# The first layer norm of a two-layer decoder trunk: tile 0 alone on VectorE, tile 1 on ScalarE and GpSimd, norm vectors spread by TensorE, first weight block in quarters

## The reference

```python
def _layer_norm(x, g, b):
    mu = jnp.mean(xf, axis=-1, keepdims=True)
    var = jnp.mean(jnp.square(xf - mu), axis=-1, keepdims=True)
    y = (xf - mu) * lax.rsqrt(var + LN_EPS)
    return (y * g + b).astype(x.dtype)

x = _layer_norm(x, ln_in_g, ln_in_b)
for l in range(DEPTH):
    hcat = jnp.einsum('bsd,de->bse', x, w_in[l])   # D_IN = 6662 columns
    ...
```

## Time and profile before

| | |
|---|---|
| median of three runs | 871.85 us |
| the profiled execution | 871.45 us |
| its span, first to last instruction | 869.7 us |
| mean granted TensorE clock | 0.998 |

### The profile page before, as it was taken

How to read it: one execution, slowest core, us unless ns; L and a number is a source line. 1 busy time by engine, 2 the same in 40 slices (tenths; PEclk the granted TensorE clock), 3 DMA queues, 4 the chain that set the end, 5 groups by cost and what they waited for, 6 DMA issues and landing times.

```text
span 869.7 us, 10886 instructions
## 1 busy us (share of the span) xinstructions
PE 847.2 (97%) x4280; PEld 703.0 (81%) x4280; DVE 514.9 (59%) x729; ACT 406.1 (47%) x553; POOL 56.4 (6%) x86
## 2 busy tenths in 40 slices
PE   7999999999999999999999999999999899999995
PEld 7878888888877888888878889888888688888884
DVE  6755465555896555445675656463778764555436
ACT  6665555453355344444337655564443444343430
POOL 0022321000000000000000414200000000000000
PEclk9999999999999999999999999999999999999999
DMA  7774443356537655665437443435754576556501
GB/s 273 240 260 135 133 133 122 122 184 238 183 130 244 217 184 194 193 194 162 141 110 241 145 158 100 135 114 184 236 176 139 189 250 208 188 177 194 194 1 49
DMA packets 93618, 149.36 MB, mean 172 GB/s; under 512 B 3584, under 2 KB 52992, under 8 KB 93568
## 3 DMA queue, kind: packets, MB, share of 16 engines
q1 hardware_dynamic: 93568, 148.67, 52.4%
HBM read 147.60 MB, written 1.05 MB: 171 GB/s over the span
## 4 chain that ended last, share of the span: by engine, by line
PE 88%; DVE 8%; DMA 2%; ACT 2%; issue 1%; DVEq 0%; ACTq 0%
PE bank L1116 78%; DVE w_lo L913 3%; PE bank L1131 3%; PE bank L1175 3%; PE bank L1207 2%; DMA raw<-in_w_in 1%; PE bank L1195 1%; PE bank L1141 1%; DVE stats L1031 1%; ACT w_hi L802 1%; DVE x L1076 1%; DVE x L1028 1%; DVE x L1073 1%; DVE act_lo L919 1%; DVE newton L1048 0%
## 5 line engine op out<-in xcount | busy, mean ns | idle before, releaser
L913 DVE TENSOR_TENSOR w_lo<-raw,w_hi 128x2048 fp32r<-128x2048 f32 (+3 forms) x143 | 309.5, 2169 | 91.5 <-ACT w_hi L802 91.0
L1116 PE MATMUL bank<-w_hi,act_hi 128*128 128x512 f32 (+2 forms) x864 | 341.8, 396 | 0.6 <-DVE act_lo L919 0.6
L1116 PE MATMUL bank<-w_hi,act_lo 128*128 128x512 f32 (+2 forms) x864 | 332.4, 385 | 0.0
L1116 PE MATMUL bank<-w_lo,act_hi 128*128 128x512 f32 (+2 forms) x864 | 331.4, 384 | 0.0
L802 ACT CAST w_hi<-raw 128x2048 fp32r<-128x2048 f32 (+3 forms) x143 | 257.5, 1803 | 123.9 <-PE bank L1116 98.8
L1116 PEld LDWEIGHTS bank<-w_hi,act_lo 128*128 128x128 f32 x864 | 162.3, 188 | 32.9
L1116 PEld LDWEIGHTS bank<-w_hi,act_hi 128*128 128x128 f32 x864 | 162.6, 188 | 30.3 <-DVE act_lo L919 0.9
L1116 PEld LDWEIGHTS bank<-w_lo,act_hi 128*128 128x128 f32 x864 | 162.8, 188 | 28.6
L1116 PE MATMUL bank<-w_hi,y_hi 128*128 128x512 f32 x240 | 95.2, 397 | 0.0
L1116 PE MATMUL bank<-w_hi,y_lo 128*128 128x512 f32 x240 | 93.7, 390 | 0.0
L1116 PE MATMUL bank<-w_lo,y_hi 128*128 128x512 f32 x240 | 93.5, 390 | 0.0
(11 more groups left out here) (96 smaller groups left out, 576.5 us busy)
## 6 DMA issues: line engine op xcount, KB each, us to landing
raw<-in_w_in SPq DMA_DIRECT2D x47, 1024.0 KB, 5.2
raw<-in_w_gate SPq DMA_DIRECT2D x44, 512.0 KB, 3.9
raw<-in_w_up SPq DMA_DIRECT2D x44, 512.0 KB, 5.0
raw<-in_w_down SPq DMA_DIRECT2D x22, 1024.0 KB, 4.9
raw<-in_w_o SPq DMA_DIRECT2D x8, 1024.0 KB, 5.2
raw<-in_w_in SPq DMA_DIRECT2D x4, 768.0 KB, 4.5
raw<-in_w_pa SPq DMA_DIRECT2D x4, 768.0 KB, 4.3
raw<-in_w_pc SPq DMA_DIRECT2D x4, 768.0 KB, 4.4
```

The lines of the kernel that those rows point to most:

```text
L913: dve.tensor_tensor(weights(w_lo, i, HI_SLOTS), weights(raw, i, RAW_SLOTS), weights(w_hi, i, HI_SLOTS).bitcast(F32), ALU.subtract).then_in ...
L1116: ins = pe.matmul(bank[use[0]][:, 0:width], a, w[:, k, c0:c0 + width], start=start and k == 0 and p == 0, stop=stop and k == nk - 1 and p ...
```

## The change

The plan's beginning is written anew. SyncE loads tile 0, the two norm vectors as one row on one partition, the first quarter, the identity, the second quarter, tile 1, the third and fourth quarter, and then piece 4. TensorE runs 8 dummies, then multiplies a row of ones (one partition) with the norm vectors, 512 columns at a time, which puts gain and bias on all partitions in banks 2 to 5 (plain float32). VectorE computes tile 0 alone: the statistics, one inverse root by `pow` on GpSimd (with one Newton step behind it), gain and bias from the banks. Tile 1 is summed by ScalarE with an accumulating ACTIVATE, its mean, variance, root and shift are made by nine instructions of one column on GpSimd, ScalarE squares and then normalises it, and VectorE applies gain and bias (`second_affine`). The step "affine", the two broadcast loads and the ACTIVATEs of L815 are gone. The first block is four pieces of quarter size; all later pieces are the same as before under a number one higher.

```diff
-WARM = (48, 16)
+WARM = (8, 6, 14)
+QUARTERS = 4
...
+def slot_before(i, n_slots):
+
+    if i < QUARTERS // 2 + n_slots:
+        return None
+    if i < QUARTERS + n_slots:
+        return 2 * (i - n_slots - QUARTERS // 2) + 1
+    return i - n_slots
...
-    statistics({t: None for t in range(TT)}, 1)
-    scale(0)
+    norm[0] = TT
+    norm_n.update({t: t + 1 for t in range(TT)})
+    spread_rows = [[bank(2 + 2 * a + j) for j in range(2)] for a in range(2)]
+    plan.append(("warm", WARM[0]))
+    plan.append(("spread_rows", spread_rows))
+    plan.append(("warm", WARM[1]))
+    plan.append(("first_norm", spread_rows))
     split_hi()
     split_lo()
     split_hi()
-    plan.append(("warm", WARM[0]))
+    plan.append(("second_sum",))
     turn_x(0, 0)
     split_lo()
-    plan.append(("warm", WARM[1]))
-    scale(1)
+    plan.append(("second_squares",))
+    turn_x(0, 1)
     split_hi()
     split_lo()
-    turn_x(0, 1)
+    plan.append(("second_rows",))
+    split_hi()
+    split_lo()
+    plan.append(("warm", WARM[2]))
+    plan.append(("second_affine", spread_rows))
...
                     if (c, t) == (0, 1):
-                        for _ in range(HI_SLOTS - 2):
+                        split_hi()
+                        turn_x(1, 0, 1)
+                        for _ in range(HI_SLOTS - 3):
...
+            sp.dma_start(x[0][:, :], d["x"][0:P, :]).then_inc(x_loaded[0], 16)
+            sp.dma_start(norm_rows, d["norms"]).then_inc(norms_loaded, 16)
+            norms, put_off = TT, None
...
+                    if i == 0:
+                        sp.dma_start(tables[:, 0:P], d["tables"][:, 0:P]).then_inc(ident_loaded, 16)
                     if i == 1:
-                        sp.dma_start(tables[:, 0:P], d["tables"][:, 0:P]).then_inc(ident_loaded, 16)
-                        sp.dma_start(norm_cols[:, :, :].rearrange("p a k -> p (a k)"), d["norms"]
-                                     ).then_inc(norms_loaded, 16)
+                        sp.dma_start(x[1][:, :], d["x"][P:2 * P, :]).then_inc(x_loaded[1], 16)
 
                     if put_off is not None:
                         put_off -= 1
                         if put_off == 0:
                             load_gain_bias(norms // TT)
                             put_off = None
-                    if i == 4:
-                        load_gain_bias(0)
...
+                elif step[0] == "first_norm":
+                    pool.wait_ge(var_ready, 1)
+                    pool.tensor_tensor(rstd[:, 0:1], var_eps[:, 0:1], exponent[:, :], ALU.pow).then_inc(root_ready, 1)
+                elif step[0] == "second_sum":
+                    pool.wait_ge(sum_ready, 1)
+                    pool.tensor_scalar(neg_mean[:, :], row_sum[:, :], -1.0 / D_MODEL, None,
+                                       ALU.mult).then_inc(mean_ready, 1)
+                elif step[0] == "second_squares":
+                    v, r, h, z = (m[:, 1:2] for m in (var_eps, rstd, half_var, newton))
+                    pool.wait_ge(squares_ready, 1)
+                    link(pool.tensor_scalar(v, square_sum[:, :], 1.0 / D_MODEL, LN_EPS, ALU.mult, ALU.add))
+                    link(pool.tensor_tensor(r, v, exponent[:, :], ALU.pow))
+                    link(pool.tensor_scalar(h, v, -0.5, None, ALU.mult))
+                    link(pool.tensor_tensor(z, r, r, ALU.mult))
+                    link(pool.tensor_tensor(z, z, h, ALU.mult))
+                    link(pool.tensor_scalar(z, z, 1.5, None, ALU.add))
+                    link(pool.tensor_tensor(r, r, z, ALU.mult))
+                    pool.wait_ge(mean_ready, 1)
+                    pool.tensor_tensor(shift[:, :], neg_mean[:, :], r, ALU.mult).then_inc(shift_ready, 1)
...
-                    if src == "first":
-                        if idx == 1:
-                            act.wait_ge(norms_loaded, 16)
-                        source_rows = first_rows[dk // 4]
-                        if t:
-                            act.wait_ge(drained[first_use[dk][0]], first_use[dk][1])
-                        first_use[dk] = (b, n)
-                        for k in range(nk):
-                            ins = act.activation(source_rows[:, k * P:(k + 1) * P], bank[b][:, k * P:(k + 1) * P],
-                                                 ACT.Identity, bias=norm_cols[:, 1, dk + k:dk + k + 1],
-                                                 scale=norm_cols[:, 0, dk + k:dk + k + 1])
-                        link(ins)
...
+                elif kind == "second_sum":
+                    act.wait_ge(x_loaded[1], 16)
+                    act.activation(merged[1][:, :], x[1][:, :], ACT.Identity,
+                                   accum_out=row_sum[:, :]).then_inc(sum_ready, 1)
+                elif kind == "second_squares":
+                    act.wait_ge(mean_ready, 1)
+                    act.activation(merged[1][:, :], x[1][:, :], ACT.Square, bias=neg_mean[:, :],
+                                   accum_out=square_sum[:, :]).then_inc(squares_ready, 1)
+                elif kind == "second_rows":
+                    act.wait_ge(squares_ready, 1)
+                    act.wait_ge(shift_ready, 1)
+                    act.activation(merged[1][:, :], x[1][:, :], ACT.Identity, bias=shift[:, :],
+                                   scale=rstd[:, 1:2]).then_inc(centred, 1)
...
-                elif kind == "affine":
-                    _, t, (b, n) = step
-                    dve.wait_ge(gb_loaded, 32)
-                    dve.wait_ge(filled[b], n)
-                    link(dve.tensor_tensor(x[t][:, :], x[t][:, :], gain_bias[:, 0, :], ALU.mult))
-                    link(dve.tensor_tensor(x[t][:, :], x[t][:, :], gain_bias[:, 1, :], ALU.add))
...
+                elif kind == "first_norm":
+                    _, (gain, bias) = step
+                    dve.wait_ge(x_loaded[0], 16)
                     for nh in range(2):
-                        xh = x[t][:, nh * NW:(nh + 1) * NW]
-                        dve.tensor_scalar(xh, xh, mean_var[:, t, 0:1], rstd[:, t:t + 1], ALU.subtract,
-                                          ALU.mult).then_inc(x_ready, 1)
+                        mark(dve.bn_stats(stats[:, 0, nh, :], x[0][:, nh * NW:(nh + 1) * NW]))
+                    settle()
+                    link(dve.bn_aggr(mean_var[:, 0, :], stats[:, 0, :, :]))
+                    dve.tensor_scalar(var_eps[:, 0:1], mean_var[:, 0, 1:2], LN_EPS, None,
+                                      ALU.add).then_inc(var_ready, 1)
+                    mark(dve.tensor_scalar(half_var[:, 0:1], mean_var[:, 0, 1:2], LN_EPS, -0.5, ALU.add, ALU.mult))
+                    for nh, (b, n) in enumerate(gain):
+                        xh = x[0][:, nh * NW:(nh + 1) * NW]
+                        dve.wait_ge(filled[b], n)
+                        mark(dve.scalar_tensor_tensor(out=xh, in0=xh, scalar=mean_var[:, 0, 0:1], in1=bank[b][:, :],
+                                                      op0=ALU.subtract, op1=ALU.mult))
+                    settle()
+                    dve.wait_ge(root_ready, 1)
+                    link(dve.scalar_tensor_tensor(out=newton[:, 0:1], in0=rstd[:, 0:1], scalar=half_var[:, 0:1],
+                                                  in1=rstd[:, 0:1], op0=ALU.mult, op1=ALU.mult))
+                    link(dve.scalar_tensor_tensor(out=rstd[:, 0:1], in0=newton[:, 0:1], scalar=1.5, in1=rstd[:, 0:1],
+                                                  op0=ALU.add, op1=ALU.mult))
+                    for nh, (b, n) in enumerate(bias):
+                        xh = x[0][:, nh * NW:(nh + 1) * NW]
+                        dve.wait_ge(filled[b], n)
+                        dve.scalar_tensor_tensor(out=xh, in0=xh, scalar=rstd[:, 0:1], in1=bank[b][:, :], op0=ALU.mult,
+                                                 op1=ALU.add).then_inc(x_ready, 1)
+                    dve.wait_ge(x_ready, 2)
+                elif kind == "second_affine":
+                    _, (gain, bias) = step
+                    dve.wait_ge(centred, 1)
+                    for nh in range(2):
+                        half = slice(nh * NW, (nh + 1) * NW)
+                        dve.tensor_tensor(x[1][:, half], merged[1][:, half], bank[gain[nh][0]][:, :],
+                                          ALU.mult).then_inc(drained[gain[nh][0]], 1)
+                        dve.wait_ge(drained[gain[nh][0]], gain[nh][1])
+                        dve.tensor_tensor(x[1][:, half], x[1][:, half], bank[bias[nh][0]][:, :],
+                                          ALU.add).then_inc(x_ready, 1)
+                    dve.wait_ge(x_ready, 2 * TT)
+                    for spare, (b, n) in zip((shift, square_sum), bias):
+                        dve.memset(spare[:, :], 0.0).then_inc(drained[b], 1)
...
+                elif kind == "spread_rows":
+                    pe.wait_ge(norms_loaded, 16)
+                    pe.wait_ge(ones_ready, 1)
+                    for a, uses in enumerate(step[1]):
```

(26 more changed lines are left out.)

88 lines of the change are left out of this document (44 added, 44 removed).

## The result

The changed kernel takes 877.92 us (median; 876.05 to 878.88), the kernel before, timed beside it, 871.98 us. The ratio is 1.0063, with a 95% interval of 1.0051 to 1.0076: 0.63% slower. It is estimated from the runs of both kernels and is not the quotient of the two medians, which lie 5.9 us apart. The profiled execution took 877.86 us with a span of 876.1 us, 6.4 us more than the span before (869.7). The mean granted clock of the four executions differs (0.994, 0.991, 0.996 and 0.998 for 876.1, 877.1, 876.2 and 874.3 us of span); the profiled one is the first.

The account below looks back on a forecast made before the run. TensorE, busy 97% of the span, bounds the kernel, so tile 1's first product with weights was the mark: 3.9 us later, less 1.7 given back, +2.2 on the 871.85 median makes 874.1 us; range 870.8 to 876.8.

Parts of the forecast that it names:

- Tile 0, the spreading: Start, TensorE's four norm-vector products: over at 10.05 us, first product with weights near 13.3 instead of 14.21.
- I take the same 3.9 us from there: Spreading products: TensorE's clock stays low for 3.9 us from 4.65, when unbroken work starts; later products run faster.
- Tile 1's chain: Tile 1 on ScalarE, GpSimd, VectorE: shift ready at 17.4, first product at 26.3 instead of 22.37, 3.9 us later.
- The two meetings: GpSimd's tile 1 steps stopped by VectorE's `w_lo` of the second and third quarter, costing 0.55 and 1.15 us.
- The clock falls in the holes: Rival, chance 0.10: TensorE's clock drops in its waits between about 17.6 and 26.3 us, losing 1.95 us: 876.0.
- the hole of 1.44 us: Kernel before: TensorE's wait ending at 19.15; the 0.22 us spacing behind it showed no fall of the clock.
- Given back: Ahead of the attention scores: the later tile 1 start closes two existing TensorE waits, returning 1.7 us.
- the holes: Kernel before: TensorE waits of 0.29 us at 54.08 and 1.41 us at 58.95, forecast to close.
- GpSimd's first arithmetic late: Rival, chance 0.07: GpSimd's first arithmetic is delayed at tile 0's root; 5 us late gives 876.8 us.
- The range: Forecast span of the whole time, 870.8 to 876.8 us, leaving out the faster case and most of the late GpSimd.
- the likeliest case: Whole kernel: tile 1's delay less the closed waits, +2.2 us, 874.1 us; chance 0.43, own range 873.1 to 875.5.
- the supply of weights: Chain of `w_lo` steps and loads ending in the waits at 54 and 59 us; reaches the scores by 60.65 at latest.

Follow-up runs that it names:

- a1_first: Changed kernel with 24 dummies instead of 8 at the start, ahead of the norm-vector products: 876.82 us, ratio to the kernel before 1.0046.
- d1: Changed kernel, still 8 dummies first, with the norm-vector products made over all 128 rows instead of one: 875.9 us, ratio to the kernel before 1.0053.
- b1: Changed kernel with norm-vector products over 128 rows instead of one and 24 dummies first instead of 8: 874.83 us, ratio to the kernel before 1.0034.
- b2: Changed kernel without the five GpSimd instructions of tile 1's Newton step: 875.73 us, ratio to the kernel before 1.0043.
- a3: Changed kernel with the fourth quarter's cast and low part ahead of ScalarE's third pass over tile 1: 875.68 us, ratio to the kernel before 1.0036.
- a2: Changed kernel with 14 dummies ahead of the fourth quarter's products and 14 behind tile 1's turns: 876.27 us, ratio to the kernel before 1.0041.
- c1: Changed kernel with 128-row norm-vector products, 24 dummies first, and the fourth quarter's cast and low part ahead of ScalarE's third pass: 871.31 us, ratio 0.9992.
- b3: Kernel before with only the first block's weights in four quarter pieces instead of two quarters and a half: 871.38 us, ratio 0.9997.
- b4: Changed kernel: 24 dummies first, fourth quarter's cast before third pass, tile 1's turned halves before whole-piece cast, 6 and 8 dummies around its turns: 874.71 us.
- c3: Changed kernel: 128-row products, 24 dummies first, fourth quarter's cast before third pass, no tile 1 Newton step, turned halves before cast, 6 dummies between turns: 870.63 us.

## Why the prediction was wrong

- *Tile 0, the spreading.* Here is the step that failed: "I take the same 3.9 us from there", by which the clock rises at 8.55 and the products end at 10.05. It assumed that any matmul does for the clock what the dummies of the earlier trace rows did. The clock stayed low under the one-row products and fell under them in a1_first; over 128 rows it rose (d1) or stayed high (b1). The price of one product at the low level (1.7, measured 2 x 0.85) and at the high level (0.9, measured 2 x 0.43) was right. The first product with weights came at 16.87, not 13.3. That delays the turned half 0 and with it the squares (14.31 for 12.1) and gives 2.2 of the 2.4 us by which tile 1 was later than forecast. Where the clock was up, in b1_rows, the squares start at 12.35.
- *Tile 1's chain.* Right in mechanism and size: from the end of the squares to the shift 4.0 us forecast, 4.15 measured (15.55 to 19.70); from the shift to tile 1's first product 8.9 against 9.0. The two meetings were priced at 1.7; one of 1.0 (`half_var`, 1.25 for 0.2) and one of 0.4 (`var_eps`, 0.69 for 0.26) came. That the chain is on the path is shown by b2, that ScalarE's order puts the rest behind it by a3.
- *The clock falls in the holes.* A rival with 0.10, 1.95 us. It happened, 1.79 us by the changed kernel against the kernel before and 1.65 by a2. The row that spoke against it, the spacing behind the hole of 1.44 us, was one shorter wait. The Trainium skill, "TensorE: Matmul & The Clock Gate", section "HAM oscillation — how this bites in real kernels", describes such falls between groups of matmuls; the trace of the changed kernel agrees with it (0.50 from 30 to 32 us, behind waits of 2.24, 0.49 and 2.10 us). It does not come each time: c1 had waits of 2.02 and 0.67 us and read 1.00.
- *Given back.* 1.70 forecast, 2.03 measured; the holes did close. This bound is why b3 gains nothing and b4 less than forecast.
- *GpSimd's first arithmetic late.* It did not happen: the first `pow` starts 0.15 us after the variance and takes 0.57 us (5.96). The Trainium skill, "GPSIMD Engine Reference", section "2.1 Instruction dispatch", names about 6 us for the first call of freshly loaded code; no such wait shows here.
- *The range.* It ended at 876.8, the price of a late GpSimd, and the clock low to 16 us had no place in it: the likeliest case with that (+2.4) and the fall (+1.8) gives 871.85 + 2.2 + 4.2 = 878.2. The two clock effects are separate. b1_rows has the first gone and still the fall (0.50 from 28 to 30 us), a2_holes the other way round. Each alone would have stayed within the range (876.5 and 875.9); that both might come was not added up.

Left open: why one-row products do not keep the clock up (a narrower ones matrix, or fewer columns, was not tried), why the fall in the waits comes in some executions and not in others, and why the two loads on c3's chain take 1.1 us longer.

## What to carry to other kernels

Where a product on one row stands at the start or in a wait, don't count it as cover for TensorE's clock: price what stands behind it at the low level, or fill its other rows with zeros, which cost two memsets of 0.9 us here and gave 3 us at the first product with weights and 2 us of the time. When a norm is moved to slower engines, read each queue from its last link to the next product: two plan entries in the other order were worth 3 us of tile 1's start and 2 us of the time, more than any instruction in the chain. And look for the next bound first: of what tile 1 gained, everything past the supply of weights came back as waits ahead of the scores, 35 to 37 us later.

## What the runs showed of the hardware

- A float32 product by 512 columns (two instructions) took 1.7 us at the low clock, over one row (changed kernel) as over 128 (d1_rows_only), and 0.86 us at the high clock, over one row (a1_first, its first instructions) as over 128 (b1_rows): the rows make no difference to its length, only to the clock.
- The granted clock column read 1.00 up to 16 us of the changed kernel, where the counts (11 in 2 us) say 1.2 GHz; in a1_first it read 0.50 for about the same counts (12). In all 14 traces it reads 1.00 until the clock has first risen, and shows the low level only for a fall after that; ahead of the first rise the spacing of the matmuls is the only witness.
- GpSimd instructions on one column took 0.19 to 0.26 us, `pow` 0.57, with 0.08 between linked ones. One that starts while a `w_lo` runs ends with it or just after: 1.25 under the `w_lo` of 17.01 to 18.24. No `pow` started under a `w_lo`, so nothing here shows whether it is stopped too; in c1 it started in the gap between two of them, ran on under the second and still took 0.57. The Trainium skill, "SBUF — State Buffer", section "Who interferes with whom", has the rule that such pairs exclude each other; these rows agree.
- ScalarE's read of an accumulator took 0.19 us, of which about 0.1 shows behind the pass.
